# Strassen pairs of a transformer kernel: high and low inputs in one 512-column matmul, products kept in shared banks, one weight sum made by an adding DMA

## The reference, cut to what matters

```
hn = rms_norm(x, norm_gain)
proj = hn @ w_in                       # its last 3 * 2048 columns are gate_logits
g = sigmoid(gate_logits.reshape(b, s, 3, 2048))
y = g[:, :, 0] * ua + g[:, :, 1] * ub + g[:, :, 2] * uc
out = x + y @ w_out
```

## Time and profile before

| | us |
|---|---|
| median of 3 runs | 2147.54 |
| lowest and highest | 2146.1 and 2147.6 |
| span of the profiled execution | 2144.3 |
| gate pairs (21), from and to | 702.8 to 1126.3 |
| output pairs (7), from and to | about 2000 to 2141 |

### The profile page before, as it was taken

One profiled execution on the slowest core, in us unless ns is written; L12 is line 12 of the kernel. 1 busy time (PEld: TensorE's weight loads), 2 busy tenths in 40 slices (PEclk: granted clock), 3 DMA queues, 4 the chain that ended last, 5 costly groups with the idle time before them and its releaser, 6 DMA issues.

```text
span 2144.3 us, 35680 instructions
## 1 busy us (share of the span) xinstructions
PE 2114.5 (99%) x12168; PEld 1835.5 (86%) x12168; DVE 1638.5 (76%) x2684; ACT 920.1 (43%) x1581; POOL 76.9 (4%) x145
## 2 busy tenths in 40 slices
PE   7899999999999999999999999999999999999999
PEld 6788888788887999999998888888787888888999
DVE  6887877775667888888886666666868776777887
ACT  6434454433335444444444444444545444223433
POOL 0000000000000000000000000000000000010000
PEclk9999999999999999999999999999999999999999
DMA  9766432565544343343333222222222223665543
GB/s 381 266 243 234 178 96 97 208 219 191 177 144 132 123 144 128 121 142 131 119 105 119 89 88 88 88 90 87 70 81 78 89 89 121 205 213 181 193 142 109
DMA packets 85935, 310.76 MB, mean 145 GB/s; under 512 B 9765, under 2 KB 12213, under 8 KB 77505
## 3 DMA queue, kind: packets, MB, share of 16 engines
q1 hardware_dynamic: 71568, 258.24, 35.6%
q0 software_dynamic: 11520, 46.68, 6.2%
q10 hardware_dynamic: 2738, 4.47, 0.6%
HBM read 284.41 MB, written 24.94 MB: 144 GB/s over the span
## 4 chain that ended last, share of the span: by engine, by line
PE 83%; DVE 6%; ACT 3%; DVEq 3%; DMA 2%; issue 1%; ACTq 0%
PE bank L425 18%; PE bank L427 18%; PE bank L426 18%; PE bank L1172 9%; PE bank L1174 9%; PE bank L1173 9%; DVE w_lo L419 2%; ACT w_hi L409 1%; PE bank L554 1%; PE bank L585 1%; DMA w_raw<-stream 1%; DMA front_raw<-stream 1%; PE bank L567 1%; DVEq L414 1%; ACT probs L637 1%
## 5 line engine op out<-in xcount | busy, mean ns | idle before, releaser
L425 PE MATMUL bank<-x_hi,w_hi 128*128 128x512 f32 x2000 | 789.1, 395 | 3.6 <-ACTq L1357 1.2
L427 PE MATMUL bank<-x_hi,w_lo 128*128 128x512 f32 x2000 | 779.1, 390 | 0.0
L426 PE MATMUL bank<-x_lo,w_hi 128*128 128x512 f32 x2000 | 778.6, 389 | 0.0
L419 DVE TENSOR_TENSOR w_lo<-w_raw,w_hi 128x512 fp32r<-128x512 f32 x468 | 324.2, 693 | 315.6 <-ACT w_hi L409 286.6
L409 ACT ACTIVATE w_hi<-w_raw 128x512 fp32r<-128x512 f32 x468 | 295.9, 632 | 572.4 <-PE bank L427 477.0
L425 PEld LDWEIGHTS bank<-x_hi,w_hi 128*128 128x128 f32 x2000 | 375.4, 188 | 94.4 <-issue 8.9
L1172 PE MATMUL bank<-x_hi,pw_hi 128*128 128x256 f32 x1568 | 444.0, 283 | 0.8 <-issue 0.7
L1173 PE MATMUL bank<-x_lo,pw_hi 128*128 128x256 f32 x1568 | 443.7, 283 | 0.0
L1174 PE MATMUL bank<-x_hi,pw_lo 128*128 128x256 f32 x1568 | 443.7, 283 | 0.0
L427 PEld LDWEIGHTS bank<-x_hi,w_lo 128*128 128x128 f32 x2000 | 375.4, 188 | 79.6
L426 PEld LDWEIGHTS bank<-x_lo,w_hi 128*128 128x128 f32 x2000 | 375.7, 188 | 75.4 <-issue 0.2
(11 more groups left out here) (214 smaller groups left out, 1840.5 us busy)
## 6 DMA issues: line engine op xcount, KB each, us to landing
w_raw<-stream SPq DMA_DIRECT2D x234, 512.0 KB, 3.7
pw_raw<-stream SPq DMA_DIRECT2D x112, 512.0 KB, 4.6
wmod<-w_mod_rows SPq DMA_DIRECT2D x32, 1024.0 KB, 6.7
front_raw<-stream SPq DMA_DIRECT2D x16, 1024.0 KB, 9.0
wmod<-w_mod_rows POOLq DMA_DIRECT2D x16, 1024.0 KB, 5.2
sig_store<-logits POOLq DMA_DIRECT2D x45, 256.0 KB, 2.5
sig_back<-sig_store SPq DMA_DIRECT2D x8, 768.0 KB, 5.9
gate_sig<-sig_store SPq DMA_DIRECT2D x7, 768.0 KB, 5.8
```

The source lines that it names most:

```text
L419: nc.vector.tensor_tensor(w_lo[:, q, :], raw_quarter(s), w_hi[:, q, :].bitcast(F32), ALU.subtract).then_inc(lo_ready, 1)
L425: nc.tensor.matmul(bank_ap[:, :tokens], hi, x_hi[:, kx, :], start=start, stop=False)
L426: nc.tensor.matmul(bank_ap[:, :tokens], hi, x_lo[:, kx, :], start=False, stop=False)
L427: return nc.tensor.matmul(bank_ap[:, :tokens], lo, x_hi[:, kx, :], start=False, stop=stop)
```

## The change

1. x1 and x2 become one tensor each, [128, 2, 16, 512], high part first. One matmul of 512 columns takes the high weights by the 256 tokens of the high and the 256 of the low input, and writes them to the two halves of a bank. The matmul of the low weights adds 256 columns to the first half. So a product's value is the sum of the two halves of its bank, and they are added ("folded") later.
2. The matmuls themselves add products 0, 2, 4 and 6 of a pair up in the bank `chain` (one of three in turn) and products 3 and 5 in `side`; product 1 stands alone in `single`. ScalarE copies the intermediate values of the bank before the next product goes on top (`copied`, at products 1, 3 and 4, and `chain_half` at product 0 of the next pair); VectorE adds (`added`, 512 columns, steps 4, 5 and 6), folds (`folded`, steps 4, 5, 6; `chain_folded`, step 2 of the next pair) and multiplies by r (`times_r`, steps 0 and 2). The scheme is taken with a21 and a22 negated, so that every sum is an addition: x2 changes sign (scale -1 on ScalarE, a scalar_tensor_tensor on VectorE for the low part), the second output tile comes out negated, and its sigmoid takes scale -1.
3. The factors are now a11, a12, s2, s1, s3, s4, a22 with s1 = a21 + a22, s3 = a21 + a11, s2 = s1 + a11, s4 = s2 + a12. Each has one buffer. SyncE loads a11, a21 into s1, a12, a21 again into s3, and a22. GpSimd waits for the first a21 and issues a DMA that adds a22 into s1. VectorE makes s3 in step 0, s4 in step 1, and s2 of the next pair in step 5.
4. The final operations and stores of the last pair are written anew.

The stream of weights that the host lays out is not touched. Cut to its core:

```diff
+            def load_factors(pair, which):
...
+                if "s1" in which:
+                    if first:
+                        sp.wait_ge(t_ready, tiles + 2)
+                    else:
+                        sp.wait_ge(pw_lo_ready, ((pair - 1).times(7) + 4).value())
+                    sp.dma_start(s1[:, :], block_in_stream(pair, 1, 0)).then_inc(s1_loaded, 16)
...
+            every = ("a11", "s1", "a12", "s3", "a22")
+            load_factors(At(0), every)
+            with steps(sp, 1, PAIRS) as i:
+                load_factors(At(0, 1, i), every)
...
+                to, x, odd, tokens = [
+                    (chain[f.j], x1, 0, lower), (single, x1, 1, lower), (chain[f.j], x2, 1, upper), (side, x2, 0, upper),
+                    (chain[f.j], x2, 0, lower), (side, x1, 1, upper), (chain[f.j], x2, 1, lower)][f.o]
...
-                    nc.tensor.matmul(to, hi, x_hi[:, 2 * k + odd, tokens], start=k == 0, stop=False)
-                    nc.tensor.matmul(to, hi, x_lo[:, 2 * k + odd, tokens], start=False, stop=False)
-                    mm = nc.tensor.matmul(to, lo, x_hi[:, 2 * k + odd, tokens], start=False, stop=k == 7)
+                    begins = k == 0 and f.o in (0, 1, 3)
+                    nc.tensor.matmul(to[:, :].rearrange("p (a t) -> p a t", a=2), hi, x[:, :, 2 * k + odd, tokens],
+                                     start=begins, stop=False, skip_group_check=True)
+                    mm = nc.tensor.matmul(to[:, :HALF], lo, x[:, 0, 2 * k + odd, tokens], start=False, stop=k == 7,
+                                          skip_group_check=True)
...
             def act_product(l, i=None):
...
+                if f.o == 0 and f.pair.positive() and not (i is None and l == PRODUCTS):
+                    chain_half(f.pair, (f.j - 1) % 3, result[:, 1, :] if l >= PRODUCTS else logits[1])
+                if f.o == 1:
+                    copied(f, first_term, chain[f.j], f.pair.times(4) - 2)
+                if f.o == 3:
+                    copied(f, second_sum, chain[f.j], f.pair.times(4))
+                if f.o == 4:
+                    copied(f, fifth_term, side, f.pair.times(4) - 1)
                 factor_hi(f.ahead(2))
...
             def dve_product(l, i=None):
...
+                dve.drain()
+                if f.o >= 4:
+                    dve.wait_ge(product_done, f.n.value())
...
+                elif f.o == 0 and f.pair.positive():
+                    times_r(0)
...
+                if f.o == 0:
+                    dve.wait_ge(s3_loaded, (f.pair + 1).times(16).value())
+                    nc.vector.tensor_tensor(s3[:, :], s3[:, :], a11[:, :], ALU.add).then_inc(s3_summed, 1)
+                if f.o == 1:
+                    weight_sum(f.ahead(4))
...
+                elif f.o == 2 and f.pair.positive():
+                    chain_folded(f.pair, (f.j - 1) % 3, logits[1])
+                    dve.drain()
+                    times_r(1)
                 if f.o == 4:
+                    added(f, first_term, 1, single)
+                if f.o == 5:
+                    added(f, fifth_term, 3, chain[f.j])
+                    weight_sum(f.ahead(4))
                 if f.o == 6:
+                    added(f, second_sum, 2, side)
                 factor_lo(f.ahead(2))
+                if f.o == 4:
+                    folded(f, 0, lower, first_term)
+                if f.o == 5:
+                    folded(f, 1, upper, fifth_term)
+                if f.o == 6:
+                    folded(f, 0, upper, second_sum)
...
+            def sum_s1(pair):
+
+                pool.wait_ge(s1_loaded, (pair + 1).times(16).value())
+                pool.dma_start(s1[:, :], block_in_stream(pair, 1, 1), accum_op=ALU.add).then_inc(s1_summed, 16)
+
+            def gate_pair(q, i=None, sums=True):
+
+                pair = At(q, 3, i)
+                if q or i:
+                    n, b = At(2 + 2 * ((q - 1) // 3), 2, i), (q - 1) % 3
+                    sigmoid_store(pair.times(2) + 1, n, b, 0)
+                if sums:
+                    sum_s1(pair + 1)
+                if q or i:
+                    sigmoid_store(pair.times(2) + 2, n + 1, b, 1)
```

More of the change, by code:

```diff
@@ L309, in program @@
         misc = bank[7]
[L310 removed]
+        single, side, chain = bank[3], bank[4], bank[5:8]
         consts_loaded, cols_loaded = sem("consts_loaded"), sem("cols_loaded")
@@ L456, in ahead, with block_in_stream @@
                 return Factor(l, self.n.i)
[L458 to L465, removed]
+        def block_in_stream(pair, row, column):
+            return stream[(pair.times(2) + (PANELS + row)).pick(), :, column * 8 * P:(column + 1) * 8 * P].rearrange(
+                "a p n -> p (a n)")
         def rstd_guess(act, width, m):
@@ L1967, in weight_sum @@
             def weight_sum(f):
-                a11, a12, a21, a22 = (raw_of(f, a)[0] for a in range(4))
-                dve.drain()
+                if f is None:
+                    return
+                once = (f.pair + 1).times(16).value()
                 if f.o == 2:
-                    for a in (2, 3):
-                        dve.wait_ge(raw_of(f, a)[1], raw_of(f, a)[2])
-                to, one, two, op = {2: (w_sum[0], a21, a22, ALU.add), 3: (w_sum[1], w_sum[0], a11, ALU.subtract),
-                                    4: (w_sum[0], a12, w_sum[1], ALU.subtract), 5: (w_sum[1], a11, a21, ALU.subtract)}[f.o]
@@ new lines, in weight_sum, with added @@
+                    dve.wait_ge(s1_summed, once)
+                    nc.vector.tensor_tensor(s2[:, :], s1[:, :], a11[:, :], ALU.add).then_inc(w_sum_made, 1)
+                else:
+                    dve.wait_ge(a12_loaded, once)
+                    nc.vector.tensor_tensor(s4[:, :], s2[:, :], a12[:, :], ALU.add).then_inc(w_sum_made, 1)
+            def added(f, term, copies, source):
+                dve.wait_ge(term_copied, (f.pair.times(4) + copies).value())
+                nc.vector.tensor_tensor(term[:, :], term[:, :], source[:, :], ALU.add).then_inc(row_read, 1)
@@ new lines, in chain_folded, with times_r, with_x @@
+            def chain_folded(pair, j, into):
+                dve.wait_ge(term_copied, pair.times(4).value())
+                nc.vector.tensor_tensor(into[:, :HALF], into[:, :HALF], chain[j][:, HALF:], ALU.add).then_inc(row_read, 1)
+            def times_r(slot):
+                nc.vector.tensor_tensor(logits[slot][:, :], logits[slot][:, :], r_both[:, :], ALU.mult).then_inc(logits_made, 1)
+            def with_x(n, half=None):
+                half = slice(0, T) if half is None else half
+                dve.wait_ge(x_back_loaded[n % 2], 16 * (n // 2 + 1))
+                return nc.vector.tensor_tensor(result[:, n % 2, half], x_back[:, n % 2, half], result[:, n % 2, half],
+                                               ALU.subtract if n % 2 else ALU.add)
```

320 lines of the change are left out of this document (171 added, 149 removed).

## The result

The changed kernel takes 2230.91 us (median of four runs, 2228.67 to 2236.04) against 2146.97 us (four runs of before, 2146.1 to 2147.6): a ratio of 1.0395, 95% interval 1.038 to 1.041. The forecast was 2183.5, with a range up to 2214. The sign is right, the size is not: +84 us where +36 was forecast. The profiled execution took 2231.27 us, its span is 2229.7 us, 85.4 more than the span before.

The account below looks back on a forecast made before the run. PE bounds the kernel before; after, the loop through the accumulating transfer decides: 26 A - 101.3 with A = 5.2 gives +33.9, plus 1.8, so 2147.5 + 36 = 2183.5 us. Own range 2153 to 2212, whole range 2127 to 2214.

Parts of the forecast that it names:

- The loop: One s1 buffer ties VectorE's part, a21's load and the accumulate in series: 16.5 + A a pair, 21.7 us, against 20.16 before.
- A: Time of GpSimd's accumulating transfer of a22 into s1, once a pair: taken as 5.2 us.
- Ends 3.5 and 7: Bounds for A: 3.5 us for a plain 512 KB GpSimd transfer; about 7 from the longest queued sigmoid store, 7.1.
- the load 3.8: SyncE's plain load of a21 into s1, inside the loop: 3.8 us from issue to landing.
- +1.8 for the out pairs: x_back loads ahead of s1 in SyncE's queue: about 0.3 us in each of 6 out pairs, +1.8 us.
- its part of the loop: VectorE from the s2 sum to the low part of s1: 11.7 us, with 0.4 us less in 12 written-out pairs.
- One wait that I had ruled out: Second row's sigmoid store, queued behind the accumulate on GpSimd: its reader was held to come later than the s2 sum.
- The first pair of each stretch has its sum loaded early: First pairs of the two product stretches do not go round the loop: 19.5 us each, 39 in all.
- 0.360 us becomes 0.2267 + 0.120 = 0.3467: PE's step over k with one 512- and one 256-column matmul: 20.9 us less over 28 pairs if PE stays the bound.
- The estimate of 4.4 us for A: Skill-page estimate of the accumulate: 2.0 fixed + 2 x 1.2 us, adding free, second source read costing.
- Rival 1: Accumulate hidden, s1 ready before the s2 sum, faster: 2133 us, PE limit 2126.6; chance 0.17 together with another rival.
- Rival 4: Accumulate far slower than two reads, A = 7: +81, 2228 us; chance 0.14 with anything beyond.

Follow-up runs that it names:

- e3: Changed kernel with two s1 buffers in turn, loaded and summed one pair ahead, accumulate kept and issued before the first row's sigmoid store: 2139.73 us, ratio 0.9968.
- e1: Changed kernel with the transfer into s1 as a plain copy, the addition of a21 and a22 left out: 2193.66 us, ratio 1.0221.
- e7: Changed kernel with the accumulate issued as two transfers of 256 KB, one after the other on the same queue: 2267.3 us, ratio 1.056.
- e4: Changed kernel with SyncE's load of a22 moved behind the landing of the accumulate: 2227.72 us, ratio 1.038.
- e6: Kernel of e3 with the two matmuls of a step over k turned round from each product's second step on: 2135.81 us, ratio 0.9946.

## Why the prediction was right in its sign and wrong in its size

- **The loop**, the heart of the argument, is there as written: same members, same order, VectorE waiting once a pair at the s2 sum. e3 opens it with all else kept and the loss is gone. The step without which the sign would have been wrong was to ask when the one s1 buffer comes free, not how busy the DMA engines are.
- **The term that failed is A, "Ends 3.5 and 7; I take 5.2, nearest to the 1 MB row plus a little of the neighbours".** It is 6.56 us, and 26 x 1.36 = 35 of the 48 us that the forecast fell short. The mechanism was right and the size was not: my bounds held it, but the point was taken by bytes read. A plain transfer of 512 KB in that place takes 5.4 already (e1), and the add comes on top with 1.1. By e7 an estimated 2.9 to 3.5 us of the accumulate don't go with its bytes. Of the two neighbours that I named, the a22 load adds nothing (e4); the s3 load was not tested and goes with the long ones. The first end, 3.5, was interpolated from transfers elsewhere in the kernel.
- **"the load 3.8"** was one row, and a quick one: the earlier trace rows had 4.6 as the median. It is 4.46, +17 us over 26 pairs, of which my +1.8 for the out pairs had foreseen a part. Taking the median would have given +36 + 21 = +57.
- **VectorE**: 11.23 us for its part of the loop against 11.7; the first number includes what the written-out pairs save, for which I had taken 0.4 us off 12 pairs. 26 x 0.47 - 12 x 0.4 = 7.4 us less than forecast. 5 of them are the first turn of each stretch, which is short (8.7 and 8.9 us); the other turns take 11.5 in the register loop and 11.2 written out, near to the forecast.
- **One wait that I had ruled out**: "its reader is the fold at the end of step 5 of that pair". In the first pair the store behind the accumulate on GpSimd is that of the first row's buffer, whose reader is the fold at the end of step 4. It lands at 724.66; VectorE's fold has to wait for it 7.1 us, PE 6.7, once. It puts off the next s2 sum by 3.1 us beyond the landing of the accumulate, which the table's last term holds.
- **"The first pair of each stretch has its sum loaded early (19.5 us each, 39 in all)"** was 10.6 us short: outside the 26 turns the two stretches take 49.6 us. From the last s2 sum to the last matmul it is 23.6 us in both. PE can begin the pair only 2.6 us after the sum, behind the low part, and then needs 21.0 for its 19.4, since it goes on at the lower clock. And the first accumulate of the output pairs took 8.58 us, not early enough: 2.5 us from the first matmul to the first s2 sum.
- These add up to the loss in the stretches: 35.3 for A, 17.2 - 1.8 for the load, -7.4 for VectorE, -2.0 for the small terms, -1.3 because I had rounded the loop's 16.45 to 16.5, +10.6 for the ends, and -1.1 because the stretches before took 565.6 us, not 564.5. That is 49.5, all of the difference between the 85.2 us lost and the 35.7 forecast.
- **PE**: "0.360 us becomes 0.2267 + 0.120 = 0.3467" is right for about two thirds of the undisturbed steps; the others take 0.3533, a gain of 6.7 ns a step and not 13.3. In the changed kernel PE is not the bound and this costs nothing; in e3 it is the difference between 19.41 and 19.80 us a pair, some 8 us over the gates. Its fastest run, 2133.0, is 6.7 us from its median, which would fit, but that run has no trace. The estimate by the Trainium skill (TensorE: Matmul & The Clock Gate, Back-to-back issue gap), 2.5 ns a matmul, which the page gives for a matmul by itself, is under both measured gains.
- **The estimate of 4.4 us for A by the Trainium skill** (Collectives: The Full Stack, The bandwidth ceiling: the fold count and why AG ≠ RS ≠ AR, with DMA: Bandwidth & Descriptors, Anatomy of one DMA) is 2.2 us under the measurement. What it says of the add fits e1 well enough: not the adding but the second read is the cost, 1.2 us by the estimate, and the transfer takes 1.1 us more with the add, each packet 0.33 in place of 0.16 us. But 0.36 of the 1.1 is about what GpSimd's longer issue takes, and whether the packets' time is the read alone these runs don't separate. The estimate's miss is in the rest: 2.0 + 1.2 = 3.2 us for the plain transfer, which took 5.4 in this place.
- **Rival 1** (hidden accumulate, 2133) is what e3 builds, at 2140, and e6, at 2136. **Rival 4** (A = 7, 2228) came nearest to the result, with 0.14; the range ended at A = 6.5, just short of it. With ends of 3.5 and 7 and no row of the thing itself, the range should have gone to the upper end; by the same sum that is 2230, and the measured time would still lie a hair above, since the load and the ends were too short as well.

## What to carry to other kernels

Before a sum moves from an engine to an accumulating transfer, write down the whole turn of its buffer: last read, wait, load, wait, accumulate, next read. Here it was 23.1 us against a pair of 20.2, with the DMA engines half idle; a second buffer made the same transfers free in all pairs but the first of the output. And where the trace has no row of an operation that sits in such a loop, carry the upper bound into the range, since each microsecond counts once per turn (26 us here).

## What was not expected of the hardware

- PE's alternating 512- and 256-column matmuls ran with one of two steps, 0.3467 or 0.3533 us, held through up to 1158 steps without a stall (e3, 708.93 to 1118 us), in the same code.
- After most of its longer stalls PE goes on at its lower clock for a while. The windows of the changed kernel before and after the wait at 931.83, and the timeline behind that wait:

```profile
912.00:924.00 12.00, 12.00 (x69) 10.42 (x69) 9.66 (x11) 7.41 (x10) 2.00 (x3) 1.00 0.67 202
924.00:934.00 10.00, 7.45 (x37) 6.18 (x37) 5.34 (x7) 2.73 (x4) 0.00 (x0) 0.89 0.45 125
```

```profile
931.83 0.79 PE L1191 MATMUL bank<-x,pw_hi 128*128 128x512 f32 x1 [2.55 <-DVE pw_lo L2018]
932.42 0.41 PE L1193 MATMUL bank<-x,pw_lo 128*128 128x256 f32 x1
932.63 0.63 PE L1191 MATMUL bank<-x,pw_hi 128*128 128x512 f32 x1
933.06 0.41 PE L1193 MATMUL bank<-x,pw_lo 128*128 128x256 f32 x1
933.27 0.63 PE L1191 MATMUL bank<-x,pw_hi 128*128 128x512 f32 x1
```

The granted clock falls from 1.00 to 0.89, and five steps take 0.64 to 0.80 us, the 1.2 GHz level, before the step is back at 0.35. This happens 17 times in the two stretches, behind stalls of 1.8 to 6.7 us, but not behind every such one: the stall of 2.9 us that ends at 1049.21 has no slow step after it. The slow steps hold 32 us more than steps of 0.35 would, which is most of why PE's busy time grew with less work. In the turns of the loop it fell into slack, since VectorE's part was not longer than forecast; in the last pair of each stretch it cost 1.6 us.
- GpSimd's issue of the accumulate takes 0.90 us, against 0.54 for a store and for the same transfer without the add (e1), and from the landing to that issue it takes 0.69 us in the pairs of the register loop and 0.29 in those written out.
